# Sums of squares by matrix product with one column (two in the heads) instead of 128

## The reference

```python
def rmsnorm(x, g):
    xf = x.astype(jnp.float32)
    y = xf * lax.rsqrt(jnp.mean(xf * xf, axis=-1, keepdims=True) + EPS)
    return (y * g.astype(jnp.float32)).astype(x.dtype)
```

## Time and profile before

| | us |
|---|---|
| median of 3 runs | 2585.95 (2584.3 to 2587.71) |
| profiled execution | 2584.89 |
| its span | 2582.8 |
| PE busy | 2504.9 |
| PEld busy | 2125.8 |
| DVE, ACT, POOL busy | 1486.1, 674.3, 1713.9 |

### The profile page before, as it was taken

The page is one execution under the profiler, slowest core; times in us unless marked ns, Lnnn a source line. Parts: engine busy times, 40 slices in busy tenths (PEclk is TensorE's granted clock), DMA queues, the critical chain, the costliest instruction groups (busy, mean ns, idle before and its releaser), DMA issues.

```text
span 2582.8 us, 35867 instructions
## 1 busy us (share of the span) xinstructions
PE 2504.9 (97%) x12919; PEld 2125.8 (82%) x12919; DVE 1486.1 (58%) x3290; ACT 674.3 (26%) x1215; POOL 1713.9 (66%) x1299
## 2 busy tenths in 40 slices
PE   6999999999999999999999999999999999999999
PEld 5876788888876676777788999999999978888887
DVE  7779521212413324433478897787778566666666
ACT  2137310101233424334110111111112233323332
POOL 3831476777552253474756678999997688888885
PEclk9989999999999999999999999999999999999999
DMA  9430122222221021221233348999997999999995
GB/s 381 188 114 17 50 98 98 84 98 95 88 77 49 33 71 48 82 98 66 83 121 113 127 171 300 330 336 356 366 348 271 343 368 346 352 345 352 351 350 207
DMA packets 134362, 501.85 MB, mean 194 GB/s; under 512 B 11232, under 2 KB 53600, under 8 KB 102752
## 3 DMA queue, kind: packets, MB, share of 16 engines
q1 hardware_dynamic: 70576, 311.71, 32.9%
q0 software_dynamic: 36864, 134.23, 13.7%
q10 hardware_dynamic: 26800, 54.32, 5.5%
HBM read 447.79 MB, written 52.43 MB: 194 GB/s over the span
## 4 chain that ended last, share of the span: by engine, by line
PE 74%; POOL 8%; DMA 7%; DVE 4%; issue 4%; ACT 1%; SPq 0%; ACTq 0%; DVEq 0%; POOLq 0%
PE banks L609 9%; PE banks L611 9%; PE banks L610 9%; PE banks L973 5%; PE banks L975 5%; PE banks L974 5%; PE banks L1058 3%; PE banks L1059 3%; PE banks L1060 3%; POOL W_lo L544 3%; DMA raw<-weights 3%; PE banks L778 3%; PE banks L796 2%; PE banks L1033 2%; POOL W_lo L467 2%
## 5 line engine op out<-in xcount | busy, mean ns | idle before, releaser
L492 POOL TENSOR_TENSOR W_lo<-raw,W_hi 128x512 fp32r<-128x512 f32 x376 | 495.9, 1329 | 0.0
L495 POOL TENSOR_TENSOR beat<-zero 128x1 f32<-128x1 f32 x94 | 19.2, 204 | 637.4 <-PE banks L611 208.5
L973 PE MATMUL banks<-A_hi,W_hi 128*128 128x384 f32 x1024 | 379.8, 371 | 1.1 <-issue 1.1
L975 PE MATMUL banks<-A_hi,W_lo 128*128 128x384 f32 x1024 | 345.9, 338 | 0.0
L974 PE MATMUL banks<-A_lo,W_hi 128*128 128x384 f32 x1024 | 344.3, 336 | 0.0
L467 POOL TENSOR_TENSOR W_lo<-raw,W_hi 128x2048 fp32r<-128x2048 f32 x65 | 299.6, 4609 | 5.2
L609 PE MATMUL banks<-A_hi,W_hi 128*128 128x512 f32 x680 | 268.4, 395 | 4.9 <-issue 4.9
L611 PE MATMUL banks<-A_hi,W_lo 128*128 128x512 f32 x680 | 265.6, 391 | 0.0
L610 PE MATMUL banks<-A_lo,W_hi 128*128 128x512 f32 x680 | 265.4, 390 | 0.0
L487 POOL CAST W_hi<-raw 128x512 fp32r<-128x512 f32 x376 | 248.3, 675 | 0.0
L2057 DVE TENSOR_TENSOR A_lo<-arena,A_hi 128x768 fp32r<-128x768 f32 x64 | 136.9, 2140 | 164.8 <-ACT A_hi L1498 164.7
(11 more groups left out here) (315 smaller groups left out, 5982.9 us busy)
## 6 DMA issues: line engine op xcount, KB each, us to landing
raw<-weights SPq DMA_DIRECT2D x221, 1024.0 KB, 4.9
gelu_dram<-B_plain ACTq DMA_DIRECT2D x64, 384.0 KB
gates_dram<-arena ACTq DMA_DIRECT2D x48, 512.0 KB, 10.3
arena<-gelu_dram SPq DMA_DIRECT2D x32, 768.0 KB, 8.4
arena<-gates_dram SPq DMA_DIRECT2D x30, 768.0 KB, 11.1
arena<-weights SPq DMA_DIRECT2D x15, 1024.0 KB, 10.2
B_lo_plain<-weights SPq DMA_DIRECT2D x5, 1024.0 KB, 21.0
B_plain<-weights SPq DMA_DIRECT2D x4, 1024.0 KB, 17.8
```

The costliest lines, as they stand in the source:

```text
L492: return pool.tensor_tensor(W_lo[:, j, cols], raw[:, j, cols], W_hi[:, j, cols].bitcast(F32), ALU.subtract)
L973: mm(to, lh, rh, start=k == 0, stop=False)
L975: last = mm(to, ll, rh, start=False, stop=k == KD - 1)
```

## The change

The moving operand becomes one column of mean_all, and the result one column at the start of each block; in the heads the two columns 0 and 64 of mean_64, and two columns of each block. Those are the columns that ScalarE reads. Everything else stays: the stationary operands, the number and order of instructions, the semaphores, the start and stop flags, the filling products.

```diff
--- before.py
+++ after.py
@@ -673,14 +673,14 @@
                     for i, tile in enumerate((S[4], S[2], S[3])):
                         take(squares_added) if i == 0 else take(norm_square, (KD - 1, 1)[i - 1])
                         for q in range(blocks):
-                            last = mm(bank[4 + b][:, P * q:P * q + P], tile[:, P * q:P * q + P], mean_all,
+                            last = mm(bank[4 + b][:, P * q:P * q + 1], tile[:, P * q:P * q + P], mean_all[:, 0:1],
                                       start=i == 0 and q == 0, stop=i == 2, skip_group_check=True)
                     last.then_inc(work_ready[b], 1)
                     return b, blocks
                 for k in range(KD):
                     take(norm_square)
                     for q in range(blocks):
-                        last = mm(bank[4 + b][:, P * q:P * q + P], S[k % 4][:, P * q:P * q + P], mean_all,
+                        last = mm(bank[4 + b][:, P * q:P * q + 1], S[k % 4][:, P * q:P * q + P], mean_all[:, 0:1],
                                   start=k == 0 and q == 0, stop=k == KD - 1, skip_group_check=True)
                     if k < 4:
                         last.then_inc(square_summed, 1)
@@ -849,7 +849,7 @@
             for i in range(4):
                 take(square_ready)
                 for q in range(QT):
-                    last = mm(head_root(b, i)[:, P * q:P * q + P], S[i][:, P * q:P * q + P], mean_64,
+                    last = mm(head_root(b, i)[:, P * q:P * q + P:HD], S[i][:, P * q:P * q + P], mean_64[:, 0:P:HD],
                               start=q == 0, stop=True, skip_group_check=True)
                 last.then_inc(heads_summed if i < 3 else work_ready[b], 1)
```

## The result

| | before | with one column | ratio |
|---|---|---|---|
| median of 12 runs, us | 2585.32 (2582.20 to 2590.57) | 2599.78 (2589.32 to 2605.43) | 1.0047 (1.0038 to 1.0056) |
| profiled execution, us | 2584.89 | 2600.91 | |
| its span, us | 2582.8 | 2598.8 | |
| mean granted clock | 0.993 | 0.987 | |

The kernel is slower by half a percent, by the ratio 12.2 us (9.8 to 14.5). Every ratio here is between undisturbed runs alone; one run of 3126.92 us, with the sizes swapped, is left out for it.

A forecast was written before the change was run, and what follows sets the result against it. TensorE, with work in 97% of the span, was taken to bound the kernel. The terms 6.8 + 3.0 + 1.6 + 2.1 - 0.6 gave +12.9 us over the median of 2585.95, forecast as 2598, range 2583 to 2604.

The forecast's parts named there:

- The price of a pass: Sums of squares on TensorE: a thin pass still takes 107 to 112 ns, set by its weight load.
- Rival B: Sums of squares: passes get quicker, down to 53 ns, and the clock holds; about 7 us saved, 2579; chance 0.15.
- The tails: End of the last pass at six places: its 128 columns are gone, 0.106 us each, 0.6 us together saved.
- The clock isn't held by loads: Thin sums: weight loads alone don't keep 2.4 GHz, so the clock falls; slower case, 2590 to 2604, chance 0.60.
- rival A: Thin sums: loads hold the clock, only -0.6 us is left, 2585.3 (2584 to 2587); chance 0.25 together with C.
- the fall at 161.0: Clock drop at 161.0 us, mostly attention scores on 32 of 128 rows; taken as sign that loads don't hold the clock.
- "second": Norm at L683, 64 passes: clock falls near 678.8 after 13 passes, sums, fill and spread slow; +6.8 us.
- The head norm: L852, 32 passes: fall near 268.4 with 16 passes left, products behind slow too; +3.0 us (1.7 to 3.4).
- "mem": Norm at L683, 32 passes: fall near its end, 0.4 us in it and 1.2 in products behind; +1.6 us.
- "ffn", "final" and "peer": Three short norms, thin for 2.7 us each: at the edge of a fall, 0.7 us each, +2.1 us together.
- an unslowed load as the other bound: Pass at the low clock: taken at 219 ns, with 112 as lower bound if loads aren't slowed; "second" then 1.4 us.

The follow-up runs named there:

- the sizes swapped: Against the kernel before, the norm "second" alone loads one weight column while 128 columns move, output no longer the reference's; ratio 0.9997 (0.9987 to 1.0008).
- the heads alone: Against the kernel before, only the head norm thin (two columns, 32 passes), the same text measured twice: 1.0022 (1.0011 to 1.0034), then 1.0014 (1.0003 to 1.0025).
- few loads: Against the kernel before, "second" alone with one column per block and 14 + 8 passes instead of 64, output no longer the reference's; ratio 1.0003 (0.9992 to 1.0015).

## Why the prediction was right

**The price of a pass** (107 to 112 ns at full clock, the load's): right. 110 ns with two columns in the heads (30 passes in 3.3 us) and with one in "second" alone (21 in 2.3), 113 with 64. The Trainium skill's rule of columns / 1.2 for a load (TensorE: Matmul & The Clock Gate, "LDWEIGHTS (loading the stationary operand)", 107 ns) is borne out at 2.4 GHz. The 25 ns of "Back-to-back issue gap" isn't reached: each thin product brings its own load, and the Trainium skill says in the same section that in such a stream load and product both set the spacing, so its two rules disagree less than I had put it. Rival B, faster, fell with it.

**The tails** (-0.6 us): wrong. The end is earlier, but nothing came of it. In "ffn" ScalarE read the sums 305.36 - 302.53 = 2.83 us after their first pass instead of 304.40 - 301.46 = 2.94, so 0.11 us less, as worked out; but the spread stands behind the eight fill passes in TensorE's own order and starts 3.57 us after the first pass of the sums both times (306.10 - 302.53; before, 305.03 - 301.46). Where a fill stands between a result and its reader's reply, the result may come earlier for nothing. I had named no such cover.

**The clock isn't held by loads**: right, and rival A wrong. Shown by back-to-back loads with one column (falls) and by 128 columns with one weight column (holds); with 128 moving columns the clock never fell within "second" in eight profiles, though in one of them it was still low from "final". The row that I had built on, the fall at 161.0, could not have shown it: loads were not dense there, 15 in 3.7 us. The side was the likelier one, not a proven one.

**The terms.** "second" was put at +6.8 and is +8.2 in the profile: it was entered at half speed already, since "final" had let the clock fall at 675.8, where I had given it 13 quick passes; 209 to 219 ns for a slow pass was right (13.78 / 64 = 215). The head norm was put at 3.0, the trace has 1.6 at its place. I had the fall come in the sums, with 16 slow passes; it came behind them, at 269.6, and the products of 512 columns brought the clock back after 3.4 us. In another execution of the heads alone it was 4.9. "mem" was put at 1.6 and cost 2.8: 1.1 in its sums and the rest behind them, at half speed until 1112.7, where I had 0.4 and 1.2. "ffn", "final" and "peer" together were put at 2.1 and cost -0.1 + 0.5 + 0.8 = 1.2. The changed places add to 13.8, against 13.5 without tails. (2585.95 + 12.9 is 2598.9, so the forecast beside the runs should have read 2599, not 2598.)

**What the sum didn't have.** 3.8 of the profile's 16.0 us lie at 1563 to 1573, in the expert layer, where nothing was changed: TensorE idles 1.6 us there in both, and this time the clock fell. The profiles with 64 and 32 columns, with few loads, and the second of the heads alone have that fall too; the other eight, the kernel before among them, don't. That it goes by the execution is shown by the two of the heads alone, which are one kernel, with the fall in one and not in the other. The fall at 1144, which the profile before has and the one after has not, took 1.6 us off the difference. So the sum's 12.9 was right for the median partly by luck: its terms err by up to 1.4 us each way, and a profile has a few us of falls that come and go.

How much that is in general can be read from the runs of the kernel before that were taken beside the experiments, 91 in all, from 2579.72 to 2594.16 us. Their mean clock goes from 0.989 to 0.995, and a run is quicker by 1.7 to 1.9 us for each 0.001 more. 0.001 is some 5 us at half speed, so such a stretch costs about a third of its length on average, not half; the one at 130 is an example of one with room. Its twelve runs in the table spread over 8.4 us and those with one column over 16.1, but against the 14.4 us of those 91 that is little to go by.

## What to carry to other kernels

Here a product costs the longer of its load and its moving side. Cutting the one that hides beside the other saves nothing, and here the moving columns also hold the clock: count what moves, not how busy the engine looks. Before a matmul is made thin, look at what runs within the next microseconds behind it, for that is what pays. And see what stands between the shortened piece and the one who waits: a fill or a queue there swallows the gain. A fill that is to hold the clock must itself stand where the engine would have idled anyway.

## What the runs showed that I had not expected

64 columns did not hold the clock through "second", and filling idle time won nothing. That the low level slows weight loads as much as moving columns I had taken from a mixed row, with an unslowed load as the other bound; now it is shown with next to nothing moving, 209 ns a pass against 110 in "second" alone thin. The records of a load at both levels, kernel with one column (min/median/max ns):

```profile
L683 PEld LDWEIGHTS banks<-tab,arena x160: 187/333/339, 17.2 to 1108.1; 128*128 128x128 f32 x160
```

And one weight column with 128 moving columns kept TensorE at 2.4 GHz as the full tile did.
